# A weight stream with five raw slabs, four high buffers and a lead of three, in place of six, three and two

## What is computed

```python
for layer in range(2):                                   # first block
    x = x + hybrid_mixer(rms_norm(x), w_in[layer], ...)  # 9 projections of 1024x1024, a gated recurrence, 3 more products
    if layer == 0: x = x + swiglu(h, w1, w3, w2)         # (silu(h@w1) * (h@w3)) @ w2, width 2816
    else:          x = x + sum over 8 experts e of gate[:, e] * swiglu(h, w1[e], w3[e], w2[e])   # top 2 of 8
for l in range(2):                                       # second block
    x = x + 0.5 * rmsnorm(swiglu_ffn(...))               # width 2816
    x = x + rmsnorm(mixing_sublayer(...))                # four branches, then w_out
    x = x + 0.5 * rmsnorm(swiglu_ffn(...))
```

## Time and profile before

| | |
|---|---|
| median of 3 runs | 2809.96 us (2806.56 to 2810.63) |
| profiled execution, its own time | 2810.03 us |
| its span | 2808.3 us |
| TensorE busy in the span | 2778.6 us (99%) |
| VectorE busy | 1988.7 us (71%) |
| ScalarE busy | 1710.9 us (61%) |
| mean DMA rate | 226 GB/s |
| mean granted clock of TensorE | 0.996 of full |

### The profile page before, as it was taken

How to read it: one execution, slowest core, us unless ns; L and a number is a source line. 1 busy time by engine, 2 the same in 40 slices (tenths; PEclk the granted TensorE clock), 3 DMA queues, 4 the chain that set the end, 5 groups by cost and what they waited for, 6 DMA issues and landing times.

```text
span 2808.3 us, 33666 instructions
## 1 busy us (share of the span) xinstructions
PE 2778.6 (99%) x13016; PEld 2290.4 (82%) x13016; DVE 1988.7 (71%) x2673; ACT 1710.9 (61%) x2412; POOL 32.4 (1%) x59
## 2 busy tenths in 40 slices
PE   9999999999999999999999999999999999999999
PEld 7888888888877888888888878887788888877887
DVE  6577655656668999998998965587765554787654
ACT  6657544565657777777777764476554544665543
POOL 0000000000000000000000000000000000000000
PEclk9999999999999999999999999999999999999999
DMA  7444555544448999999999965554555555544553
GB/s 269 165 135 154 184 187 184 200 162 144 166 155 286 344 375 368 346 362 362 356 366 369 358 217 181 181 196 155 169 194 186 197 189 183 188 165 165 188 186 114
DMA packets 174468, 635.29 MB, mean 226 GB/s; under 512 B 19664, under 2 KB 19696, under 8 KB 174048
## 3 DMA queue, kind: packets, MB, share of 16 engines
q1 hardware_dynamic: 171216, 621.88, 63.6%
q0 software_dynamic: 3088, 11.21, 1.1%
HBM read 630.90 MB, written 2.11 MB: 225 GB/s over the span
## 4 chain that ended last, share of the span: by engine, by line
PE 94%; DVE 3%; ACT 2%; DMA 1%; issue 0%; SPq 0%; DVEq 0%; ACTq 0%; POOLq 0%
PE ps L1657 29%; PE ps L1659 28%; PE ps L1658 28%; PE ps L1919 2%; PE ps L1835 1%; DVE wlo L914 1%; DMA XN<-bound_rows 1%; PE ps L1745 1%; PE ps L1822 0%; PE ps L1823 0%; DVE Z L1491 0%; DMA raw<-in_W 0%; PE ps L1982 0%; DVE XN L1498 0%; ACT whi L351 0%
## 5 line engine op out<-in xcount | busy, mean ns | idle before, releaser
L914 DVE TENSOR_TENSOR wlo<-raw,whi 128x1024 fp32r<-128x1024 f32 x1182 | 1386.1, 1222 | 417.8 <-ACT whi L351 411.5
L351 ACT ACTIVATE whi<-raw 128x1024 fp32r<-128x1024 f32 x1182 | 1186.8, 1057 | 436.0 <-PE ps L1659 434.2
L1657 PE MATMUL ps<-whi,XH 128*128 128x512 f32 (+1 forms) x2064 | 816.5, 396 | 6.1 <-DVE XL L943 2.2
L1658 PE MATMUL ps<-wlo,XH 128*128 128x512 f32 (+1 forms) x2064 | 802.0, 389 | 0.0
L1659 PE MATMUL ps<-whi,XL 128*128 128x512 f32 (+1 forms) x2064 | 802.0, 389 | 0.0
L1657 PEld LDWEIGHTS ps<-whi,XH 128*128 128x128 f32 x2064 | 388.4, 188 | 92.9 <-issue 9.0
L1659 PEld LDWEIGHTS ps<-whi,XL 128*128 128x128 f32 x2064 | 388.2, 188 | 81.9
L1658 PEld LDWEIGHTS ps<-wlo,XH 128*128 128x128 f32 x2064 | 388.8, 188 | 74.7
L1657 PE MATMUL ps<-whi,XEH 128*128 128x512 f32 x704 | 281.9, 400 | 1.6 <-DVE wlo L914 1.6
L1659 PE MATMUL ps<-whi,XEL 128*128 128x512 f32 x704 | 276.0, 392 | 0.0
L1658 PE MATMUL ps<-wlo,XEH 128*128 128x512 f32 x704 | 275.0, 391 | 0.0
(11 more groups left out here) (392 smaller groups left out, 2513.2 us busy)
## 6 DMA issues: line engine op xcount, KB each, us to landing
raw<-in_W SPq DMA_DIRECT2D x1182, 512.0 KB, 4.9
XN<-bound_rows POOLq DMA_DIRECT2D x2, 1024.0 KB, 7.8
GP<-in_ffn_post_g POOLq DMA_DIRECT2D x4, 512.0 KB, 4.1
X<-in_x SPq DMA_DIRECT2D x4, 256.0 KB, 5.7
skew<-RB POOLq DMA_DIRECT2D x4, 256.0 KB, 7.3
RB<-skew POOLq DMA_DIRECT2D x8, 128.0 KB, 6.3
GP<-in_mix_post_g POOLq DMA_DIRECT2D x2, 512.0 KB, 3.9
MP<-in_pool_windows POOLq DMA_DIRECT2D x1, 768.0 KB, 7.3
```

What stands on the lines that cost most here:

```text
L351: act.activation(k.whi[:, slot, part], k.raw[:, at, part], ACT.Copy).then_inc(*k.up("act_hi"))
L914: dve.tensor_tensor(k.wlo[:, at, part], k.raw[:, at, part], k.whi[:, slot, part], ALU.subtract).then_inc(*k.up("dve_lo"))
L1657: pe.matmul(ps, xh, k.whi[:, slot, cols], start=first, stop=False)
L1658: pe.matmul(ps, xh, k.wlo[:, at, cols], start=False, stop=False)
```

## The change

Three constants change. SBUF holds nine slab-sized buffers in both kernels.

```diff
-RING = 3
-RAW = 6
-LEAD = 2
+RING = 4
+RAW = 5
+LEAD = 3
```

## The result

The changed kernel takes **2829.74 us** (median of 4 runs, 2828.40 to 2832.93), the kernel before 2809.95 beside it (2806.56 to 2810.63): a ratio of **1.0074** with the 95% interval [1.0062, 1.0086]. That is 19.8 us more, where 20.8 had been forecast. The profiled execution took 2832.93 us, 22.9 more than the profiled one of before.

The account below looks back on a forecast made before the run. TensorE was taken to bound the kernel, 94% of the chain that ended last. Terms -3.3 + 1.0 + 15.6 + 2.5 + 4.0 + 1.0 = +20.8 on 2810.0 gave 2830.8 us; range 2808 to 2846, slower 79%.

Parts of the forecast that it names:

- waits for rests, gone: TensorE's waits for a rest near 35, 535 and 868 us vanish with the third slab of lead: -3.3 us.
- start: At the kernel's start a third copy delays the split of tile 1, wanted at 19.33 us, to 20.3: +1.0 us.
- stop at group 10, 8 experts: Each expert's last group: GN stands behind a late copy, TensorE waits about 1.6 us; +15.6 us over eight experts.
- other groups: Experts' other groups have about 1.2 us margin, broken by landings above 7.9 us: +2.5 us, from nothing to 6.
- end of the experts: Last copy of the experts' stage lands late, so the scatter starts at 1634.0 instead of 1629.74: +4.0 us.
- clock after the scatter's stop: After a 5.8 us stop the eight scatter matmuls may run at 1.2 GHz: +1.0 us, between nothing and 1.6.
- DMA share that is given as 90% among the rivals: Rival that every group stops, some 80 at 0.3 us: 24 us more, 2855 us; chance 12%.
- The distance, by the clock: One slab of request-to-copy distance is worth 5.4 us in dense stages, 2.7 us among the experts; dense stages lose nothing.
- Place's wait inside the stop: After group 10, place's wait for the last turned rest would be 1.2 us, inside the stop already paid.
- The gathering and the expert's output: In the experts, these have 0.4 to 1 us left: forecast nothing, up to 3 us.
- The rival of the thinning queue: Among experts, short stops thin the DMA queue, landings shorten and group 10's stop goes: 2809 us; chance 15%.
- experts' landings that fall to 5 us: Sign against the forecast: it is wrong if these landings fall so far, or if L1919 does not wait for GN.

Follow-up runs that it names:

- the two kernels with a distance of two slabs: Kernel before with RAW = 5 alone: 2813.87 us, ratio 1.0017; kernel before with RING = 4 and RAW = 5, LEAD still 2: 2811.11 us, ratio 1.0008.
- those with a distance of one: The changed kernel, 2829.74 us, and the kernel before with RAW = 4 alone, 2881.97 us, ratio 1.0264.
- the experiment that removed the stop: Changed kernel, but in each expert's last group one copy and its rest come behind the turn and the gated product: 2831.26 us, ratio 1.0079.
- the run with the expert output ahead: Changed kernel, but in the last expert the stage's last copy and rest come behind the output's YH and YL: 2827.85 us, ratio 1.0063.

## Why the prediction was right

The sum, term by term; the profiles differ by 22.9 us.

| step of the prediction | forecast, us | after, us | from |
|---|---|---|---|
| waits for rests, gone | -3.3 | -3.3 | no such wait in the list |
| start | +1.0 | +1.6 as a stop, +0.7 left at 85 us | stop at 20.44 |
| stop at group 10, 8 experts | +15.6 | +13.7 | eight of the ten waits for GN_ |
| other groups | +2.5 | +1.9 | the other two, 1.71 and 0.23 |
| end of the experts | +4.0 | +2.7 | 4.24 less 1.56 |
| clock after the scatter's stop | +1.0 | +2.3 by 1667 us, +0.9 left at the end | lag from 22.0 to 24.3, 22.9 at the end |
| clock inside the experts | 0 | +3.2 | two falls, 8 x 0.2 us each |
| lost beside the listed idle time | 0 | +3.1 | see below |
| sum | +20.8 | +22.9, with the start at 0.7 and the scatter's clock at 0.9 | |

About 3 us of the 22.9 are in none of the stops. Most of them lie in how a stop is counted. Each matmul of a slab is 0.39 us long in the record, but under full work the next one starts 0.23 us after it; the idle time before a late matmul is counted from the end of the last one, and so leaves out 0.16 us of every stop, and the first matmuls behind it come another 0.05 late. Held against the same matmuls in the trace of before, the lag grows by 2.29 us at the stop of 2.08, by 1.81 at the one of 1.59 and by 0.43 at the one of 0.23. For the ten stops that is some 2.2 us more than their idle time. The waits that went count in the same way: ahead of the stop at 917 us the new kernel was 3.2 us early, where the rows give 2.6. A stop of 0.31 us for an earlier expert's output (YL, at 1249.64) cost 0.6, and a few gaps too short for the list cost some 0.9; one of 0.10 us ahead of 1510.98 cost 0.3.

**The number is nearer than its terms.** Five terms came out lower than forecast, by 4.2 us together (group 10 1.9, end 1.3, other groups 0.6, start 0.3, scatter's clock 0.1), and 6.3 us came from two rows that were put at nothing. That they nearly cancel is luck; the place and the size of the greatest term are not.

Three slips in the working changed little. The end of the experts adds up to 4.3 us and not 4.0 (1634.0 less 1629.74), and the sum with it to 21.1. The stop of "3.4 us" ahead of the stretch at 0.83 is one of 2.97 us in the trace, and one of 1.48 follows it before the first slow matmuls of a slab. And the DMA share that is given as 90% among the rivals is 1.0 in the earlier trace rows. The line of the 2.97, from the trace of before:

```profile
1635.03 1.23 PE L1745 MATMUL ps<-ident,X 128*128 128x128 f32 x8 [2.97 <-DVE X L1402]
```

- **The distance, by the clock.** Right, and shown: the two kernels with a distance of two slabs cost 2 and 5 us, those with a distance of one 20 (the changed kernel) and 73. That these slabs are worth 2.7 us in the experts and 5.4 elsewhere is why nothing was lost in the dense stages: at 400 to 450 us TensorE is busy throughout in both, and the work at 585 us stands 1.4 us *earlier* than before.
- **Group 10.** The eight stops are 2.08, 1.59, 1.39, 1.31, 2.27, 1.21, 2.00 and 1.84 us. The forecast for all was 1.55 plus what a landing exceeds 6.6 us by: right in the place and the number, and near in the mean (1.7 against 1.95). Too high were the sixth and the seventh, forecast at 2.75 and 2.85 from the two slowest landings of before and measured at 1.21 and 2.00; too low were the first and the fifth, forecast at 1.55: a single landing isn't repeated from one execution to the next.
- **Place's wait inside the stop.** Right, and the sharpest part of it: the experiment that removed the stop found exactly that wait, 1.2 us long, eight times.
- **The gathering and the expert's output**, "nothing, up to 3": for the gathering nothing in the changed kernel, and 4.4 us more when the stops ahead of it were gone; for the output the one stop of 0.31 us.
- **The end** was mis-sized by 1.3 us: the landing was 6.2 us and not 7.5. The stop was to be 5 to 6 us and was 4.24. The request in question was not as late as the one of before at 1617.3 us from which it was priced.
- **The clock.** The term for the scatter, 1.0, has the number by luck: the low clock lasted past the scatter's eight matmuls and had cost 2.3 us by 1667, and 1.4 of these were gone again at the end. That it would fall inside the experts was missed, 3.2 us. The prediction let the stop of 1.56 us that kept the clock stand for all of group 10, and did not ask what the longer ones would do.
- **The rival of the thinning queue** was half true. A slab's second half requested at 1016.8 us, in the stop, landed in 6.1 us and one at 1021.6 in 5.1; the one at 1025.0 took 7.3. So landings are shorter behind a stop, as that rival had it, but 7 us after the stop's end (1017.95) they were back, and the next group 10 is over 90 us away. The Trainium skill, "DMA: Bandwidth & Descriptors", "Anatomy of one DMA", fits 2.0 us plus bytes at 436 GB/s, given there for the GpSimd path; for the two halves an estimate of 4.4 us. The experts' landings come near it only behind a stop (5.1 us); those of the dense stretch do with 4.7 (median). By it no expert would have waited, and the measurement decides.

Of what would have shown the prediction wrong, experts' landings that fall to 5 us, nothing came: the median is 6.2 where it was 6.4.

## What to carry to other kernels

Count a prefetch distance from the request to the first use of the data (here the copy), in microseconds of the stage that uses data fastest, and hold it against the landing under full load; a deeper lead on the consumers' side, paid for with a buffer on the requests' side, shortens just that. A lead protects the slabs, not the other jobs in the same in-order queue: whoever stands behind the late copy is late, so list them all, since each stop that is removed shows the next. Where only two or three places gain from more lead, a different order of the work there may give the same for nothing (here 2.8 us, 0.1%). And the cost of a stop is read from the lag of the same instruction in two traces; the idle time alone leaves some 0.2 us of each stop out.

## What the hardware showed that was not expected

- TensorE's clock after a stop isn't told by the stop's length alone. In the changed kernel it fell to 1.2 GHz for some 3 us after stops of 2.00 and 2.27 us and stayed at 2.4 GHz after one of 2.08, after those of 1.2 to 1.8, and after two of 2.42 in the dense stages (2029.73 and 2610.29). The one of 2.00 us came 11.3 us after another of 1.71; whether that decided it was not tried. In the run with the expert output ahead it fell after one of 1.94 us at 1214.58. With four raw buffers TensorE waited for a rest 55 times between 880 and 1640 us, at most 2.4 us, and no stretch of 10 us there was granted under 0.99 of the clock. So 1.94 us was enough once, and 2.42 was not in another place. What decides it stays open. The stretch behind the stop of 1.94, and then the first matmul behind the one of 2.41 with four raw buffers (granted clock 1.00 from 1541 to 1546 us):

```profile
1214.60:1218.00 3.40, 3.40 (x10) 2.72 (x11) 3.40 (x4) 2.86 (x4) 0.00 (x0) 0.54 1.01 371
...
1541.11 0.50 PE L1657 MATMUL ps<-whi,XEH 128*128 128x512 f32 x1 [2.41 <-DVE wlo L914]
```

  With five raw buffers and the old lead, one of 2.47 us made it fall as well, as TensorE's matmuls in order of time show, which come 0.43 us apart from the third on:

```profile
1495.12 0.47 PE L1657 MATMUL ps<-whi,XEH 128*128 128x512 f32 x1 [2.47 <-DVE wlo L914]
1495.42 0.46 PE L1658 MATMUL ps<-wlo,XEH 128*128 128x512 f32 x1
1495.68 0.63 PE L1659 MATMUL ps<-whi,XEL 128*128 128x512 f32 x1
1496.11 0.63 PE L1657 MATMUL ps<-whi,XEH 128*128 128x512 f32 x1
```

- The slab halves' landing hardly depends on how many raw buffers are requested ahead: from 900 to 1600 us the median is 6.4 us with six, 6.5 and 6.4 with five and the old lead, 6.2 in the changed kernel, and 6.0 with four, although four fetch 336 GB/s at 1000 to 1050 us and the others 363 to 380.
